# Delta rule of a two-block kernel: the gates' product in two F32R parts, and single-head products of keys and state placed between the two units' level products

## Time and profile before

| | |
|---|---|
| median of 3 runs | 2855.25 us (2855.1 to 2857.33) |
| the profiled execution | 2856.49 us, span in the trace 2854.7 us |
| PE busy | 2725.1 us, 95% of the span |
| DVE busy | 1633.6 us, 57% |
| ACT busy | 1186.0 us, 42% |
| POOL busy | 414.6 us, 15% |
| delta rule in the trace | from about 1419 to 1893 us |

### The profile page before, as it was taken

The page is one execution under the profiler, slowest core; times in us unless marked ns, Lnnn a source line. Parts: engine busy times, 40 slices in busy tenths (PEclk is TensorE's granted clock), DMA queues, the critical chain, the costliest instruction groups (busy, mean ns, idle before and its releaser), DMA issues.

```text
span 2854.7 us, 43894 instructions
## 1 busy us (share of the span) xinstructions
PE 2725.1 (95%) x16684; PEld 2270.0 (80%) x16684; DVE 1633.6 (57%) x2852; ACT 1186.0 (42%) x2218; POOL 414.6 (15%) x620
## 2 busy tenths in 40 slices
PE   6999999999898999999999999989999998998999
PEld 4756777778757998887688888878777787987899
DVE  4565533334665657985377777773533345357665
ACT  4343422223444445346344445543322234355443
POOL 0000000000000301000066666640000000024000
PEclk9999999999999999999999999999999999999999
DMA  7263244442263453323200000032344433110453
GB/s 286 89 236 141 96 187 166 171 167 89 104 251 136 177 178 131 123 99 111 96 1 1 1 1 1 2 119 89 136 174 176 176 119 143 65 69 24 156 185 137
DMA packets 49615, 343.36 MB, mean 120 GB/s; under 512 B 5296, under 2 KB 7344, under 8 KB 9776
## 3 DMA queue, kind: packets, MB, share of 16 engines
q1 hardware_dynamic: 44960, 324.03, 30.7%
q10 hardware_dynamic: 4496, 17.15, 1.5%
HBM read 333.82 MB, written 7.34 MB: 120 GB/s over the span
## 4 chain that ended last, share of the span: by engine, by line
PE 88%; DVE 7%; ACT 3%; DMA 2%; issue 1%; DVEq 0%; SPq 0%; ACTq 0%
PE ps L595 21%; PE ps L596 20%; PE ps L597 20%; PE ps L2147 4%; PE ps L2134 3%; PE ps L788 3%; PE ps L2126 2%; PE ps L2155 2%; PE ps L843 1%; DMA ring<-in_w_dram 1%; DVE ring_rest L583 1%; PE ps L818 1%; PE ps L2089 1%; PE ps L2945 1%; PE ps L2193 1%
## 5 line engine op out<-in xcount | busy, mean ns | idle before, releaser
L595 PE MATMUL ps<-hidden_high,w_high 128*128 128x256 f32 (+1 forms) x1176 | 396.2, 337 | 10.0 <-DVE h_rest L569 6.8
L1166 ACT ACTIVATE w_high<-ring 128x2048 fp32r<-128x2048 f32 x124 | 236.9, 1910 | 382.3 <-DMA ring<-in_w_dram 257.9
L595 PE MATMUL ps<-h_high,w_high 128*128 128x512 f32 (+1 forms) x1024 | 351.1, 343 | 10.9 <-DVE h_low L569 9.5
L596 PE MATMUL ps<-h_low,w_high 128*128 128x512 f32 (+1 forms) x1024 | 347.7, 340 | 0.0
L596 PE MATMUL ps<-hidden_low,w_high 128*128 128x512 f32 (+1 forms) x1024 | 344.6, 336 | 0.0
L1659 DVE TENSOR_TENSOR mix_high<-ring,w_high 128x2048 fp32r<-128x2048 f32 x56 | 128.4, 2293 | 247.7 <-ACT w_high L1166 247.7
L597 PE MATMUL ps<-hidden_high,ring_rest 128*128 128x256 f32 (+1 forms) x872 | 265.7, 305 | 0.0
L595 PEld LDWEIGHTS ps<-hidden_high,w_high 128*128 128x128 f32 x1176 | 224.7, 191 | 43.4 <-issue 17.2
L595 PEld LDWEIGHTS ps<-h_high,w_high 128*128 128x128 f32 x1024 | 197.0, 192 | 39.5 <-issue 19.3
L1659 DVE TENSOR_TENSOR ring_rest<-ring,w_high 128x2048 fp32r<-128x2048 f32 x68 | 157.2, 2312 | 122.3 <-ACT w_high L1166 122.3
L596 PEld LDWEIGHTS ps<-h_low,w_high 128*128 128x128 f32 x1024 | 197.0, 192 | 19.6
(11 more groups left out here) (476 smaller groups left out, 6151.8 us busy)
## 6 DMA issues: line engine op xcount, KB each, us to landing
ring<-in_w_dram SPq DMA_DIRECT2D x302, 1024.0 KB, 4.9
z_spill<-arena ACTq DMA_DIRECT2D x16, 256.0 KB, 2.0
arena<-z_spill SPq DMA_DIRECT2D x2, 2048.0 KB, 11.0
C<-in_first_dram ACTq DMA_DIRECT2D x1, 2432.0 KB, 11.1
X<-in_x_dram ACTq DMA_DIRECT2D x1, 2048.0 KB, 13.2
x_spill<-X ACTq DMA_DIRECT2D x1, 2048.0 KB, 10.9
X<-x_spill SPq DMA_DIRECT2D x1, 2048.0 KB, 7.7
C<-in_third_dram ACTq DMA_DIRECT2D x1, 2048.0 KB, 8.6
```

The source lines that it names most:

```text
L595: ins = nc.tensor.matmul(out_, w_high, high, start=first, stop=False)
L596: nc.tensor.matmul(out_, w_high, rest, start=False, stop=False)
L1166: nc.scalar.activation(W_HIGH[:, (j + 1) % 2, :], ring[:, s], ACT.Copy).then_inc(sems["w_high"], 1)
```

```diff
+            AFTER = same_place.enter_context(nc.sbuf_tensor("after_exact", [P, 256], F32R))
...
+        G_HIGH, G_REST = UQ2[:, 24:24 + P], TG[:, 0, :]
+        GATE_PARTS = [[RING_REST[:, (RULE_END - 1) % RING, at:at + T2] for at in (1024 * u, 1024 * u + T2)] for u in range(2)]
...
             def exps():
                 act.wait_ge(filled[4], v.filled(4, BANK4.index("running")))
+                nc.scalar.activation(G_HIGH, SC[:, SG_, :], ACT.Copy)
+                nc.scalar.activation(AFTER[:], cst("after", 0, 256), ACT.Copy)
...
             def decays():
                 dve.wait_ge(freed[4], v.freed(4, BANK4.index("running") + 1))
+                nc.vector.tensor_tensor(G_REST, SC[:, SG_, :], G_HIGH.bitcast(F32), ALU.subtract)
...
                 if i:
                     pe.wait_ge(sems[f"pm{u}"], LEVELS * i)
-                nc.tensor.matmul(ps[:, 4 * u + 2, :], cst("after", d * P, d * P + P), RS[:, u, :], start=True, stop=True).then_inc(sems[f"after_gate{u}"], 1)
+                mask, (high, rest) = AFTER[:, d * P:d * P + P], GATE_PARTS[u]
+                if i:
+                    nc.tensor.matmul(ps[:, 4 * u + 2, :], mask, high, start=True, stop=False)
+                    ins = nc.tensor.matmul(ps[:, 4 * u + 2, :], mask, rest, start=False, stop=True)
+                else:
+                    ins = nc.tensor.matmul(ps[:, 4 * u + 2, :], mask.bitcast(F32), RS[:, u, :], start=True, stop=True)
+                ins.then_inc(sems[f"after_gate{u}"], 1)
...
-            def of_state(i, u, part_, b, name):
+            def of_state(i, u, part_, b, name, heads=2):
                 hp = PASSES[i][2]
-                for h in range(2):
+                for h in range(heads):
...
-                of_state(i, u, 0, 4 * u, "zs")
+                of_state(i, u, 0, 4 * u, "zs", 1)
+
+            def beside_x(i, n, u, h):
+
+                pe.wait_ge(sems[f"x_kept{u}"], LEVELS * i + n)
+                S = SS[:, bass.ds(PASSES[i][2] * 8 + (4 * u + h), 1), :].rearrange("p a b -> p (a b)")
+                nc.tensor.matmul(ps[:, 4 * u, h * P:(h + 1) * P], key_heads(i, u)[:, 1, 0:P], S, start=True, stop=True)
...
-                    for u in range(2):
-                        if n == 6 and i < LAST:
-                            after_gate(i + 1, u)
-                    for u in range(2):
-                        product(i, n, u)
+                    if n == 6 and i < LAST:
+                        after_gate(i + 1, 0)
+                    product(i, n, 0)
+                    if n < 5:
+                        beside_x(i, n, (n - 1) // 2, 3 - n % 2)
+                    if n == 6 and i < LAST:
+                        after_gate(i + 1, 1)
+                    product(i, n, 1)
...
             def gate(i, u):
 
                 d, c, hp = PASSES[i]
-                if i:
-                    pool.wait_ge(sems[f"am{u}"], i)
-                for h in range(4):
-                    ins = nc.gpsimd.tensor_scalar(RS[:, u, h * P:(h + 1) * P], cst("incl", d * P, d * P + P), col(SG_, d, c, hp, u, h), None, ALU.mult)
+                incl = cst("incl", d * P, d * P + P)
+                if i == 0:
+                    for h in range(4):
+                        ins = nc.gpsimd.tensor_scalar(RS[:, u, h * P:(h + 1) * P], incl, col(SG_, d, c, hp, u, h), None, ALU.mult)
+                else:
+                    if i > 1:
+                        pool.wait_ge(sems[f"after_gate{u}"], i)
+                    for to, part_ in zip(GATE_PARTS[u], (G_HIGH.bitcast(F32), G_REST)):
+                        g = part_[:, bass.ds(c * 32 + hp * 8 + (16 * d + 4 * u), 4)].rearrange("p (h o) -> p h o", o=1).broadcast_to([P, 4, P])
+                        ins = nc.gpsimd.tensor_tensor(heads4(to), incl.rearrange("p (o n) -> p o n", o=1).broadcast_to([P, 4, P]), g, ALU.mult)
                 ins.then_inc(sems[f"gate{u}"], 1)
...
             def within(i, u):
 
                 d = PASSES[i][0]
+                if i:
+                    pool.wait_ge(sems[f"am{u}"], i)
```

More of the change, by code:

```diff
@@ L247, in build @@
             EXPS = same_place.enter_context(nc.sbuf_tensor("exps_exact", [P, 2048], F32R))
+        with ExitStack() as same_place:
+            same_place.enter_context(nc.sbuf_tensor("below_after", [P, CCOL["after"][0]], F32))
+            AFTER = same_place.enter_context(nc.sbuf_tensor("after_exact", [P, 256], F32R))
         C = sb("C", [P, NCST])
@@ L2677, in pe_state_sums @@
                 pe.wait_ge(sems["tail"], s)
-            nc.tensor.matmul(ps[:, 0, :], cst("after", d * P, d * P + P), GK[:, t, d * 512:(d + 1) * 512], start=True, stop=True).then_inc(sems["after_sum"], 1)
+            nc.tensor.matmul(ps[:, 0, :], AFTER[:, d * P:d * P + P].bitcast(F32), GK[:, t, d * 512:(d + 1) * 512], start=True, stop=True).then_inc(sems["after_sum"], 1)
             if s:
```

## The result

| | before | after |
|---|---|---|
| median of 3 runs | 2855.25 us | 2833.43 us (2831.71 to 2833.45) |
| ratio to before, 95% interval | | 0.9919 [0.9899, 0.9938] |
| the profiled execution | 2856.49 us | 2831.71 us |
| period of a pass in its trace | 29.53 us | 28.13 us |

The change saves 21.8 us, where the forecast was 16.5. A second comparison, on another chip, gave 2834.56 against 2855.27 us, 20.7 us less, with a ratio of 0.9931 [0.9917, 0.9945]. It fell by 1.40 us, and 15 x 1.40 = 21.0 us is the gain to within the measurement.

A forecast was written before the change was run, and what follows sets the result against it. VectorE, without a hole from the value rest on, was taken to bound the tail: 1.23 - 0.05 (c) - 0.05 (e), about 1.1 us per pass, 15 times, 16.5 us; forecast 2838.8 us, range 2834 to 2851.

The forecast's parts named there:

- (a): Gates' product in level 6: one fp32 matmul of 0.86 us per unit becomes two F32R ones, 0.46 us per unit.
- (b): Keys times state: 2 of 4 matmuls leave the tail, 0.86 us per pass; the value rest starts 1.23 us earlier.
- From there it is VectorE that has no hole: Tail from the first value rest: VectorE, 12.32 us busy of 12.57, carries it, so its start sets the tail's length.
- (c): Four single-head products inserted in levels 1 to 4 fill TensorE's 0.22 us hole; 0.05 us per pass deducted, at most 0.88.
- (d): Gates on GpSimd: four tensor_scalar, 2.34 us, become two tensor_tensor of 1.04 or 1.27 us each; at 1.04 nothing stalls.
- (e): Tail: GpSimd's identity copies may delay VectorE's predicated copy, 0 to 0.3 us more; 0.05 us per pass deducted.
- (f): End of the convolution: two ScalarE copies and one VectorE subtraction, once; costed at nothing, under 1.2 us without cover.
- the forecast case: The prediction's main case, 64%: own range 2836.5 to 2843.5 us, from 15 x 1.23 to 15 x 0.78 gained.
- The stated 2834: Lower end of the forecast's whole range, 2834 to 2851 us, which leaves 18% out.
- TensorE the limit: Rival, 10%: TensorE bounds everything, so 0.86 + 0.80 = 1.66 us per pass comes back, 25 us, 2830 us.
- the levels pay: Rival, 14%: insertions push whole levels by 0.22 us four times a pass, leaving 0.3 us per pass, 4.5 us, 2851 us.
- GpSimd the bound: Rival, 8%: gates take 1.16 us more each and delay levels 4 and 6, 2.0 us per pass, 2870 us.

The follow-up runs named there:

- gates_only: The kernel after without the single heads' products, all four heads of keys and state in the tail; 2843.46 us, ratio to before 0.9958.
- qk_first: The kernel after with TensorE's order changed to both `qk` ahead of both `solve`; 2828.83 us, ratio to before 0.9907.
- gate1_late: qk_first with unit 1's gates' product moved from ahead of its level-6 product to behind keys of state; 2828.29 us, ratio to before 0.9904.
- no_insert: The kernel after with the products of keys and state for heads 2 and 3 left out of the computation; 2832.35 us, ratio to before 0.9915.
- less_after_qk: The kernel before with half of queries times state (heads 2 and 3) left out, behind the second `qk`; 2854.90 us, ratio to before 0.9997.
- gate_longer: The kernel after with a third tensor_tensor of 512 columns, its result overwritten, in each gate on GpSimd; 2853.71 us, ratio to before 0.9993.
- qk_first_again: qk_first unchanged, run again on one chip beside a repeat of the kernel after; 2828.97 us, ratio to before 0.9909.
- qk_first_before: The kernel before with both `qk` ahead of both `solve` as its only edit; 2853.84 us, ratio to before 0.9994.
- heads_only: The kernel before with only the single heads' products in the levels and less keys of state in the tail; 2845.55 us, ratio to before 0.9963.

## Why the prediction was wrong, step by step

The direction and the price of each removed instruction were right; the reading of what bounds the tail was wrong at one place, and the gain came out 5 us too small. By its own steps:

(a) **Gates' product.** 0.46 us per unit was expected. The rows give 1582.48 - 1581.93 = 0.55 and 1583.38 - 1582.84 = 0.54. The level product between them is fed in 0.36 instead of 0.45, so the pair costs what it should: 2.61 - 1.89 = 0.72 us less, and 0.08 more from the gap ahead of them, against the 0.80 of the text. gates_only: 0.80. The sum is right; that it is right to the hundredth is in part luck. The product itself was priced 0.08 to 0.09 too low, and the prediction had neither the 0.09 of the level product nor the 0.08 of the gap.

(b) **Keys of state.** 0.86 less, right. Value rest 1.23 us earlier: right, 1.23.

The failed step is the one behind it: **"From there it is VectorE that has no hole: 12.32 us busy of 12.57"**, and with it "the tail's length is set by when VectorE can start at 1594.41". The 0.25 us that lack in that window were taken as nothing. They hid two waits behind TensorE's `qk`, which the rows of before show: `first` of the units start at 1596.70 and 1597.95, each 1.25 us after the VectorE step ahead of it (the second value rest at 1595.45), while one such step takes 1.03 us when nothing holds it (qk_first). Unit 0's `first` waits for ScalarE's copy of the first `qk`, as the kernel tells it to: the copy ends at 1596.51 and `first` starts 0.19 later, the same 0.19 as in gate1_late (1585.98 to 1586.17). Unit 1's `first` waits for the second `qk` itself, which it follows by 1.12 us. After the change the first of the two waits is gone and the second stands (1586.53, the start of unit 0's `first`, to 1587.82 is 1.29). It is this second one that counts: it fixes the start of unit 1's `first` whatever unit 0's does. So the stretch up to it hung on TensorE's list, which gained 1.42 us, and not on the value rest, which gained 1.23. The text even had the number: it put the first `solve` 1.5 us earlier, which the trace confirms at 1.48, and remarked only that this would not hold VectorE up. For the kernel after, the same window of VectorE is 0.19 us shorter with nearly the same work in it (columns: length, then busy us of PE, PEld, DVE, ACT, POOL):

```profile
1584.46:1596.84 12.38, 12.03 (x82) 10.76 (x80) 12.21 (x38) 7.64 (x27) 7.56 (x10) 1.00 0.01 1
```

It is 12.21 us busy of 12.38. 1.23 + 0.19 = 1.42 is the gain of a pass.

(c) **Insertions.** Deducted 0.05, cost 0. The reason given was right in each point: the level stays at 2.65 us, and in level 1 unit 1's product is late (0.74 us behind unit 0's in after, 1568.83 to 1569.57) without anyone waiting for it; no_insert gives the zero.

(d) **GpSimd.** The gates took the low one of the two prices:

```profile
L2495 POOL TENSOR_TENSOR ring_rest<-C,uq x30: 1037/1045/1056, 1431.9 to 1828.4; 128x512 fp32r<-128x512 f32 x30
```

The median is 1045 ns for 512 columns with both operands broadcast (columns: name and count, ns shortest, median and longest, first and last start). Two make 2.09 us, against 2.34 before. The Trainium skill ("GPSIMD Engine Reference", section 3.1) gives 2.6 cycles per element for this operation, by which the prediction estimated 2.2 us for the two; the trace agrees within 6%. The distance to the transposes grew from 0.28 to 0.39 us.

(e) **The collision.** Deducted 0.05, cost 0. The identity copies still take 1.66 us beside the predicated copy of 1.40, at 1588.68 and 1588.86, the same two numbers as in the earlier trace rows. On the scale of before they start at 1597.40 and 1597.58: both moved by 1.41, where the prediction moved one by 1.5 and the other by 1.23.

(f) **Once.** Nothing that the runs could tell from zero.

So of the 5.3 us that the forecast lacks, 15 x 0.19 = 2.9 are the waits that were read as nothing, 15 x 0.10 = 1.5 the two deductions, and 0.4 the rounding of 1.13 to 1.1 us per pass; the other 0.5 is within the spread of the medians. 15 x 1.42 = 21.3 from the profiled 2856.49, less the same 1.2 us, would have given 2834.0; 2833.43 and 2834.56 were measured. The range was too narrow for a related reason: the forecast case ended at 15 x 1.23, 2836.5 us in the text (its own sum gives 2836.8), as if the value rest's gain were an upper bound. The stated 2834 goes 2.5 us beyond that, without a case that gives it, and the one case that goes further, TensorE the limit, was left outside at 10%.

Of the rivals, "the levels pay" is refuted by no_insert. "TensorE is the limit everywhere" is refuted as a whole by less_after_qk, but it was half right: the limit it names holds up to the second `qk`, which is why the truth lay between 16.5 and 25 us. "GpSimd the bound" did not happen; gate_longer shows that its mechanism exists and begins 0.29 us further on. Its price was too high: 1.13 us more per gate cost 1.37 per pass, where the text took 2.0 for 1.16. (Its scaling has a slip too: 3.14 us for 896 columns is 1.79 for 512, not 1.75.)

## What to carry to other kernels

An engine that is busy 98% of a window may still be waiting, and the missing 2% decide how much of an upstream gain gets through: list the start distances of its steps in the window and compare each with the step's unhindered length, before taking the first start as what sets the end. When an edit makes two things earlier by different amounts (here 1.23 and 1.5 us), follow both to the point where they meet and see which the later work waits for. And after such a gain look at the order once more: putting both `qk` ahead of both `solve` gave 0.03 us per pass before the change and 0.25 after it.

## What the runs showed of the hardware that was not expected

**TensorE's clock at the start of the delta rule.** In the window from 1420 to 1430 us, just behind the start of the delta rule, the granted clock (the column behind PE's busy time) was 1.00 in one execution and 0.83 in another of the same code. First qk_first, then qk_first_again:

```profile
1420.00:1430.00 10.00, 7.68 (x50) 1.00 0.00 2
```

```profile
1420.00:1430.00 10.00, 7.77 (x49) 0.83 0.00 1
```

0.83 as a mean means that part of the window ran at the lower level of 1.2 GHz and the rest at 2.4. The distance from the delta rule's first exponential to its first value rest is 22.54 us with the one and 23.71 with the other, so the clock is worth about 1.2 us there. The kernel before has 0.83 in its profile, the kernel after 1.00. That is one reason why the two profiled executions lie 24.8 us apart and the medians 21.8. What decides it stays open.

**A DMA at the end.** The transfer of z_spill, which hides the last pass's tail, took 11.78 us in the kernel after and 13.26 before. In qk_first_before and less_after_qk, which have before's list in the levels where it runs, it was 13.27 and 12.13, so it varies by 1.1 us without the change. But in the seven other runs with the change's gates and shorter tail, gate_longer apart, it was 11.70 to 11.85, while heads_only, gates_only and gate_longer had 12.14, 12.51 and 12.10. Whether the change has a part in it stays open. Its 1.5 us are a second reason why the profiled executions lie 24.8 us apart; the medians, 21.8 and 20.7 us apart, leave little room for it beside the 21.0 us of the passes. Its cause was not looked for.
